# MLP of a two-group decoder step: sample tokens computed by exact fp32 products of their own, prompt tokens in 512-column products

## The reference, cut to what matters

```python
D_FF = 4 * D_MODEL
...
        x = x + jnp.concatenate([mix, mem_out], axis=-1) @ p['w_out'][l]
        h2 = rmsnorm(x, p['norm2'][l])
        x = x + jnp.square(jax.nn.relu(h2 @ p['w_mlp1'][l])) @ p['w_mlp2'][l]
```

## Time and profile before

| | |
|---|---|
| median of 3 runs | 1286.4 us (1285.06 to 1288.59) |
| profiled execution, its own time | 1290.19 us |
| its span (first to last instruction) | 1288.2 us |
| TensorE matmul busy | 1220.3 us, 9556 records |
| TensorE weight load busy | 1169.2 us |
| DVE / ACT / POOL busy | 584.3 / 409.1 / 356.7 us |
| mean granted TensorE clock | 0.972 |

### The profile page before, as it was taken

The page is one execution under the profiler, slowest core; times in us unless marked ns, Lnnn a source line. Parts: engine busy times, 40 slices in busy tenths (PEclk is TensorE's granted clock), DMA queues, the critical chain, the costliest instruction groups (busy, mean ns, idle before and its releaser), DMA issues.

```text
span 1288.2 us, 23147 instructions
## 1 busy us (share of the span) xinstructions
PE 1220.3 (95%) x9556; PEld 1169.2 (91%) x9556; DVE 584.3 (45%) x867; ACT 409.1 (32%) x754; POOL 356.7 (28%) x290
## 2 busy tenths in 40 slices
PE   6998999999999999999999888699999999999994
PEld 5877999999999999998799655699999999999994
DVE  7676444333333333446635867545333333333334
ACT  6544342212212112334412456433211211211221
POOL 3363024205205205320062200013402512502524
PEclk9999999999999999999999889599999999999997
DMA  7623422232322332232344546023222323222211
GB/s 277 210 85 107 124 97 82 84 97 82 85 97 82 88 94 82 83 90 80 135 128 119 202 149 212 1 66 95 86 82 85 96 83 90 91 85 88 90 50 70
DMA packets 37056, 132.97 MB, mean 103 GB/s; under 512 B 4226, under 2 KB 5122, under 8 KB 36322
## 3 DMA queue, kind: packets, MB, share of 16 engines
q1 hardware_dynamic: 35858, 123.42, 30.6%
q0 software_dynamic: 1104, 8.15, 2.2%
HBM read 121.18 MB, written 7.03 MB: 100 GB/s over the span
## 4 chain that ended last, share of the span: by engine, by line
PE 88%; DVE 7%; ACT 2%; issue 1%; DMA 0%; DVEq 0%; POOL 0%; SPq 0%; ACTq 0%
PE psum L432 81%; DVE inv_rms L1040 1%; DVE weights_split L1021 1%; PE psum L572 1%; PE psum L483 1%; ACT weights_split L760 1%; PE psum L497 1%; DVE tiny L1128 1%; PE psum L534 1%; PE psum L508 1%; PE psum L554 1%; PE psum L528 0%; PE psum L582 0%; PE psum L512 0%; DVE probs_heads L1107 0%
## 5 line engine op out<-in xcount | busy, mean ns | idle before, releaser
L432 PE MATMUL psum<-operand_b,weights_split 128*128 128x272 f32 x4416 | 562.6, 289 | 3.9 <-DVE weights_split L1021 3.7
L432 PEld LDWEIGHTS psum<-operand_b,weights_split 128*128 128x128 f32 x4416 | 556.7, 189 | 8.8 <-DVE weights_split L1021 4.7
L432 PE MATMUL psum<-operand_a,weights_split 128*128 128x272 f32 (+1 forms) x4116 | 529.7, 291 | 23.4 <-DVE weights_split L1021 18.3
L432 PEld LDWEIGHTS psum<-operand_a,weights_split 128*128 128x128 f32 x4116 | 523.4, 191 | 29.1 <-issue 21.9
L760 ACT ACTIVATE weights_split<-weights_raw 128x1024 fp32r<-128x1024 f32 (+1 forms) x186 | 192.6, 1035 | 392.1 <-PE psum L432 392.1
L1021 DVE TENSOR_TENSOR weights_split<-weights_raw,weights_split 128x1024 fp32r<-128x1024 f32 (+1 forms) x186 | 239.8, 1289 | 135.3 <-ACT weights_split L760 135.2
L1412 POOL TENSOR_TENSOR squares<-staging 128x544 f32<-128x544 f32 x64 | 76.3, 1193 | 469.8 <-ACT operand_a L806 207.6
L1075 DVE TENSOR_TENSOR residual<-psum,residual 128x544 f32<-128x544 f32 x48 | 34.8, 725 | 175.9 <-PE psum L432 175.9
L1056 DVE SCALAR_TENSOR_TENSOR staging<-psum,inv_rms 128x544 f32<-128x544 f32 x56 | 40.6, 725 | 150.1 <-PE psum L432 150.1
L1405 POOL TENSOR_TENSOR squares_sum<-squares_sum,squares 128x544 f32<-128x544 f32 (+1 forms) x35 | 48.6, 1388 | 115.7 <-ACT squares L772 115.1
L1414 POOL TENSOR_TENSOR operand_a<-squares,operand_a 128x544 fp32r<-128x544 f32 x32 | 65.0, 2030 | 2.5
(11 more groups left out here) (201 smaller groups left out, 720.3 us busy)
## 6 DMA issues: line engine op xcount, KB each, us to landing
weights_raw<-in_weights SPq DMA_DIRECT2D x180, 512.0 KB, 3.6
cache_tiles<-in_page_k SPq DMA_DIRECT2D x16, 384.0 KB, 3.8
cache_tiles<-in_page_v SPq DMA_DIRECT2D x16, 384.0 KB, 4.0
cache_tiles<-in_mem_k SPq DMA_DIRECT2D x8, 512.0 KB, 4.7
cache_tiles<-in_mem_v SPq DMA_DIRECT2D x8, 512.0 KB, 5.9
residual<-in_x SPq DMA_DIRECT2D x1, 2176.0 KB, 11.7
out_y<-projected SPq DMA_DIRECT2D x8, 272.0 KB, 2.1
rotated<-projected POOLq DMA_DIRECT2D x4, 408.0 KB, 7.1
```

Source lines behind the costliest of these rows:

```text
L432: mm = pe.matmul(ps[:, 2 * (j % PS) + hf, 0:n], w(wr), act[:, ar, k, hf * n:(hf + 1) * n], start=(q == 0 and wr == 0 and ar == 0), stop=(q ...
```

## The change

In the 128 MLP units only, the 32 sample tokens leave the split path:

- The prompt's unit (`prompt_unit`) is 24 products of 512 columns in one PSUM bank (0 or 2).
- After each unit whose number in its half block is 0 or 4, `sample_group` computes the sample tokens of this unit and the next three: for each feature tile, four plain fp32 products with the 32 tokens as weights and the raw weight tile as moving data, written to the four column groups of bank 1. ACT copies the 32 x 4 rows out (`group_copy`), TensorE transposes them in the middle of the next unit (`sample_turn`, into bank 3), and DVE applies the ReLU and the square or adds the residual (`group_hidden`, `group_residual`).
- `weights_raw` slots are released only after the group that reads them; all loops are written out; on ACT, `high` stands ahead of the square and of `residual_tile` in all units; `hidden_rest` and the DVE and ACT work of the up units handle 512 columns.

```diff
-                while a < b and (a % RAW or a < RAW):
...
+                for u in range(a, b):
+                    load(u, u < RAW)
...
+                    if in_mlp(u - RAW):
+                        sp.wait_ge(group_mixed, group_of(u - RAW) + 1)
...
+            def prompt_unit(u, j, act, ready=None, mid=None):
+
+                pe.wait_ge(weight_lo, u + 1)
+                pe.wait_ge(unit_out, u - PS + 1)
+                for k in range(KT):
+                    if ready:
+                        ready(k)
+                    if mid and k == KT // 2:
+                        mid()
+                    for wr, ar in ((0, 0), (0, 1), (1, 0)):
+                        mm = pe.matmul(prompt_psum(j), split[:, j % HL, wr, lo_of(k)], act[:, ar, k, 0:PROMPT],
+                                       start=(k == 0 and wr == 0 and ar == 0), stop=(k == KT - 1 and wr == 1))
+                mm.then_inc(unit_done, 1)
+
+            def sample_group(u, act):
+
+                g0 = group_of(u)
+                if g0:
+                    pe.wait_ge(group_copied, g0)
+                for g in range(4):
+                    pe.wait_ge(raw_loaded[(u + g) % RAW], 16 * ((u + g) // RAW + 1))
+                for k in range(KT):
+                    for g in range(4):
+                        mm = pe.matmul(ps[32 * g:32 * g + 32, 1, 0:P], sample_of(act)[:, k, :],
+                                       raw[:, (u + g) % RAW, lo_of(k)], start=(k == 0), stop=(k == KT - 1))
+                mm.then_inc(group_mixed, 1)
+
+            def sample_turn(u):
+
+                g0 = group_of(u)
+                pe.wait_ge(group_copied, g0 + 1)
+                if g0:
+                    pe.wait_ge(group_out, g0)
+                pe.transpose(ps[:, 3, 0:P], rows_s[:, :], ident).then_inc(group_turned, 1)
...
+                        elif j == KT:
+                            ready = lambda k: pe.wait_ge(hid_lo, i * KT + (done + k + 1))
+                        mid = (lambda: sample_turn(u + j - 1)) if j % 4 == 1 else None
+                        prompt_unit(u + j, u + j, act, ready=ready, mid=mid)
+                        if i == 0 and j == 0:
                             norm_sum(r)
+                            pe.wait_ge(sample_scaled, layer + 1)
+                        if j == KT:
+                            pe.wait_ge(group_out, group_of(u + j))
+                        if j % 4 == 0:
+                            sample_group(u + j, act)
...
             def mlp(u0, hidden, r, nr, gs):
+                        high(u + j + HL)
+                        if i == 0 and j == 0:
+                            root(r)
+                        act.wait_ge(unit_out, u + j + 1)
+                        act.activation(hidden[:, 0, j, 0:PROMPT], T[:, j % TS, 0:PROMPT], ACT.Square).then_inc(hid_hi, 1)
+                        if j % 4 == 0:
+                            group_copy(u + j)
...
+            def group_hidden(u, j, hidden):
+
+                dve.wait_ge(group_turned, group_of(u) + 1)
+                own.chain(dve.scalar_tensor_tensor(out=relu_s[:, :, :], in0=group_cols, scalar=0.0,
+                                                   in1=rms[:, PROMPT:TOK].unsqueeze(1).to_broadcast([P, 4, SAMPLE]),
+                                                   op0=ALU.max, op1=ALU.mult))
+                dve.tensor_tensor(sample_of(hidden)[:, j:j + 4, :], relu_s[:, :, :], relu_s[:, :, :], ALU.mult)\
+                   .then_inc(group_out, 1)
```

More of the change, by code:

```diff
@@ L785, in residual_tile @@
                 act.wait_ge(unit_out, u + 1)
+                if in_mlp(u):
+                    act.wait_ge(group_out, group_of(u) + 1)
                 for g, dst in gs:
-                    norm_high(g, o, X[:, o, :], dst[:, 0, o, :])
+                    cols = slice(0, PROMPT if g in (G_MLP0, G_MLP1) else TOK)
+                    norm_high(g, o, X[:, o, cols], dst[:, 0, o, cols])
                 square(r, o, X[:, o, :], TOK)
-            def mlp(u0, hidden, r, nr, gs):
[L791 to L803, removed]
-                    for j in range(KT):
[L805 to L811, removed]
@@ new lines, in group_copy @@
+            def group_copy(u):
+                g0 = group_of(u)
+                act.wait_ge(group_mixed, g0 + 1)
+                if g0:
+                    act.wait_ge(group_turned, g0)
+                act.activation(rows_s[:, :], group_rows, ACT.Copy).then_inc(group_copied, 1)
+            def mlp(u0, hidden, r, nr, gs):
+                for i in range(BLOCKS):
+                    u = u0 + 2 * KT * i
+                    for j in range(KT):
+                        high(u + j + HL)
+                        if i == 0 and j == 0:
+                            root(r)
[3 more added lines that the diff above has]
+                            group_copy(u + j)
+                    for j in range(KT):
+                        high(u + KT + j + HL)
+                        if j % 4 == 0:
+                            group_copy(u + KT + j)
+                        if i == BLOCKS - 1:
+                            residual_tile(u + KT + j, j, nr, gs)
@@ L1061, in mlp @@
                 dve.wait_ge(rms_ready, r + 1)
[L1062 to L1065, removed]
-                                                 in1=halves(rms[:, :]), op0=ALU.max, op1=ALU.mult).then_inc(unit_out, 1)
-                    else:
-                        hidden(u0 + j, j, n0 + j - TS + 1)
-                    weight_rest(u0 + j + HL, (u0 + j + HL) % RAW)
@@ L1313, in _ @@
             out_units(U_OUT0, G_MLP0, A)
[L1314 removed]
+            mlp(U_MLP0, R_MLP0, G_IN1, A, B)
             inverse(R_IN1)
@@ L1418, in mlp @@
                 n0 = BLOCKS * KT * (u0 == U_MLP1)
-                with pool.Fori(0, BLOCKS) as i:
+                for i in range(BLOCKS):
                     for j in range(KT):
```

94 lines of the change are left out of this document (56 added, 38 removed).

## The result

The change makes the kernel slower: 1302.8 us, the median of 4 runs (1298.5 to 1308.07), against 1285.73 us of 4 runs of the kernel before; the ratio is 1.0135 with a 95% interval of 1.0087 to 1.0183. The forecast was 1259 us with a range of 1248 to 1290. The profiled execution took 1308.07 us (span 1306.1, 17.9 more than the span before).

The account below looks back on a forecast made before the run. TensorE, busy 95% of the span, was taken as the bound. Terms -106.8 + 67.5 + 3.5 + 6.4 + 2.3 = -27.1 us took 1286.4 to 1259.3 us, range 1248 to 1290.

Parts of the forecast that it names:

- Part 1: MLP units: 24 products of 512 columns at 0.216 us replace 48 of 272; -106.8 us over 128 units.
- Rival (a): Wide products: the fixed loss per product stays, 0.2254 us each; +28.9 us, about 1287, no change; chance 0.11.
- Rival (b): Wide products: loss in proportion to the columns, 0.236 us each; +61 us, 1318; chance 0.04.
- The bound from below: Wide products at their bare stream, 512/2.4 GHz = 0.2133 us each; put at -113 us for the units.
- Part 2: Sample groups: 32 at 2.11 us including the change of form, +67.5 us; one transposition each at 0.11, +3.5 us.
- (c): Sample groups: TensorE's instruction issue becomes the bound; 1362 us at 39 ns each, 1283 at half; chance 0.13 for slower.
- (d): Sample groups: the four column groups don't run side by side; 7 us per group, +160 us; chance 0.01.
- Part 3: First down unit of each block: TensorE waits 0.8 to 0.9 us longer for the eighth hidden tile; +6.4 us, 0 to 12.
- Part 4: Start of each MLP: second unit's transposition waits for ACT's group copy; +2.3 us, clock fall of 0 to 5 not summed.
- Costed at nothing: Later raw slot release, DVE's blocking waits, small DVE and ACT group work and the moved `residual_tile`: expected hidden, 0 us.

Follow-up runs that it names:

- the bursts: Kernel before, with bursts of 48 unread matmul records behind its last norm sum, differing in format, length or operands; 512-column fp32r took 0.227 to 0.230 us, plain fp32 0.216.
- e_aligned: Changed kernel with the MLP's prompt operands stored 512 columns apart and the sample tokens' operand behind them: 1289.66 us, ratio 1.0017 to the kernel before.
- e_both: Changed kernel with prompt operands stored 512 columns apart and each MLP's first transposition one unit later: 1285.54 us, ratio 0.9994 to the kernel before.
- e_late_turn: Changed kernel with the first transposition of each MLP in the middle of unit 2 instead of unit 1: 1297.01 us, ratio 1.0067 to the kernel before.

## Why the prediction was wrong, by its steps

**Part 1 failed**, and it alone turned the sign. Its sentence "So the loss goes where a stream is about 0.22 us long; I read it as the weight load" rested on two rows, and the loss does not go. The norm sum is plain fp32, which has 0.0025 us beyond its stream at both lengths in the bursts: it was a row of another number format. And at half clock nothing is lost at either length that the traces hold: 272 columns stand 0.2267 us apart there and 512 columns 0.4267 (the changed kernel behind its wait at 198 us), both exactly the stream, while both lose at full clock. A row at half clock could not tell what the length of the stream does. The term measured 0.2321 instead of 0.216 us, 3072 times +49.5 us: the units gave 128 x (6.02 - 5.57) = -57.6 us instead of -106.8.

Neither rival had it alone; the measured distance lies between them. Rival (a), the fixed loss that stays (0.2254 us, 1287 us), accounts for 28.9 of the 49.5 us. Of the rest, 3072 x (0.2321 - 0.2270) = 15.7 us come from where the operand's tiles begin, 544 columns apart, which the prediction did not consider and e_aligned took back (13.1 us in the medians); 4.9 us are left. On aligned tiles the distance is 0.0016 above (a), and e_aligned and e_both take 1289.7 and 1285.5. Rival (b), the loss in proportion (0.236, 1318 us), describes the kernel as it was written a little better than (a) and the aligned one not at all. It had been given 0.04 by the same norm sum ("reads as fast at full clock and loses nothing"), and the range ended with (a). The bound from below was also added up a little wrong: 24 x 0.2133 gives -115 us, not -113, and the lower end of the range would be 2 us lower. Nothing hangs on it.

**Part 2 was right.** A group was put at 2.11 us and takes 2.08, so rivals (c) and (d) fall: 128 instructions in 1.88 us show neither an issue bound nor column groups in turn. The transposition was put at 0.11 and costs 0.1.

**Part 3 had the wait but not its size.** The time from TensorE's last up product to POOL's end was expected to grow by 0.25 us; from DVE's start on it fell instead, from 337.05 - 332.17 = 4.88 to 4.65. The timeline of the kernel after:

```profile
238.80 0.69 DVE L1143 SCALAR_TENSOR_TENSOR staging<-psum,inv_rms 128x512 f32<-128x512 f32 x1 [3.19 <-PE psum L480]
238.86 1.06 ACT L817 ACTIVATE weights_split<-weights_raw 128x1024 fp32r<-128x1024 f32 x1 [3.99 <-PE psum L480]
...
239.96 1.23 DVE L1084 TENSOR_TENSOR weights_split<-weights_raw,weights_split 128x1024 fp32r<-128x1024 f32 x1 [0.46 <-ACT weights_split L817]
240.52 1.56 POOL L1482 TENSOR_TENSOR squares<-staging 128x512 f32<-128x512 f32 x1 [2.64 <-ACT operand_b L866]
242.16 1.29 POOL L1484 TENSOR_TENSOR operand_b<-squares,operand_b 128x512 fp32r<-128x512 f32 x1
```

The weight copy ahead of the square delays the square, as costed; but it also moves DVE's weight rest off POOL's subtraction (2.22 us in the earlier trace rows, 1.29 here) and onto the squaring (1.09 and 1.56). The prediction took -0.2 us on POOL for the fewer columns alone; it was -0.46. With tile eight due later (22 products of 0.232), the wait was 0.1 us and not 0.8, in the 8 blocks some 1 us together instead of 6.4.

**Part 4 was right in kind.** Both waits for the group copy are there (2.6 us and 1.1), and the clock fell in layer 0, which the sum had left out and the bounds had held. What e_late_turn takes back, 5.8 us in the medians and 5.2 in the two MLPs, is about the price of all that, against 2.3 in the sum.

**Costed at nothing**, and rightly so: no wait for a raw slot, a PSUM bank or DVE shows as idle time of L480 (0.0 in the page).

By the measured terms, in the order of the prediction's sum, it is -57.6 + 66.6 + 3 + 1 + 5 = +18 us, the span's difference.

## What to carry to other kernels

Measure the distance of the very number format that will be streamed, at the length, at the full clock and with the start addresses that it will have, before a change that trades short products for long ones; a row of another format, or of the lower clock, does not bound it. When work leaves a shared product for one of its own, count its price for each change of form and put as much behind one change as the memory holds. And when a copy changes its place, ask which two-input operation of VectorE now runs beside GpSimd.

## What the runs showed of the hardware that was not expected

- At full clock a one-pass fp32r product takes 0.012 us beyond its stream at 240 to 272 columns (0.112 and 0.1254 us) and 0.013 to 0.020 at 512 (0.227 to 0.234); plain fp32 and bf16 records of 512 streamed columns take 0.0025 (0.216). At half clock fp32r takes nothing beyond it (0.2267 for 272 columns, 0.4267 for 512). Why is open: the runs exclude the length of the load, the weights' values, the PSUM bank and the neighbours' work as the reason at 512 columns.
- The start address of a moving fp32r tile of 512 columns is worth up to 0.007 us: 0.227 with tiles 2048 bytes apart from the beginning of the operand, 0.234 with the same tiles 32 bytes further on; which address in SBUF is the good one isn't shown. At 240 columns it is worth under 0.001.
- Four column groups of plain fp32 run side by side at full rate: a round of four 128-column products takes 0.109 us per record, and the change to the narrow form and back costs 0.33 to 0.36 us, with 16 rounds between (2.08 us) or 32 (3.86 us).
- GpSimd's `tensor_tensor` takes 0.5 to 0.9 us longer beside a two-input operation of VectorE of 1.23 us.
